# Sample attention: who issues the latent pages

## The reference

```python
def one_seq(args):                                  # 8 sequences
    pages, qb, cb, rb = args
    c_past = cache_kv_latent[pages].reshape(-1, KV_LORA)      # 16 pages x 128 rows x 256
    r_past = cache_k_rope[pages].reshape(-1, QK_ROPE_DIM)
    c_all = jnp.concatenate([c_past, cb], axis=0)[None]       # and the 4 new rows
    k = mla_keys(c_all, r_all, w_uk, g_k_nope, g_k_rope)      # keys, normalised
    p = attn_probs(qb[None], k, mask)
    o_lat = jnp.einsum('bhql,blc->bqhc', p, c_all)            # weighted latent rows
    return jnp.einsum('bqhc,chv->bqhv', o_lat, w_uv)[0]
```

```python
a = gelu(einsum('thkd,td->thk', peer_u[e], hb))     # e: the picked experts of each token
return einsum('thk,thkd->td', (g * a), peer_v[e])
```

## Time and profile before

| | |
|---|---|
| median of 3 runs | 3511.48 us (3498.91 to 3511.61) |
| the profiled execution | 3516.18 us, span 3514.4 us |
| PE busy | 2845.7 us (81%) |
| DVE busy | 2707.2 us (77%) |
| ACT busy | 968.1 us (28%) |
| POOL busy | 1765.9 us (50%) |
| fetches on POOL | 1088 of 1253 (v) and 1329 (u) ns in the mean |
| sample attention | about 863 to 1262 us of the span |

### The profile page before, as it was taken

The page is one execution under the profiler, slowest core; times in us unless marked ns, Lnnn a source line. Parts: engine busy times, 40 slices in busy tenths (PEclk is TensorE's granted clock), DMA queues, the critical chain, the costliest instruction groups (busy, mean ns, idle before and its releaser), DMA issues. The chain is left out here.

```text
span 3514.4 us, 40173 instructions
## 1 busy us (share of the span) xinstructions
PE 2845.7 (81%) x12509; PEld 2094.9 (60%) x12509; DVE 2707.2 (77%) x5283; ACT 968.1 (28%) x1627; POOL 1765.9 (50%) x1379
## 2 busy tenths in 40 slices
PE   6655697886888866656629799999999999999997
PEld 3444354665333333355618677787778777777775
DVE  3237687896878847759979688888888888888886
ACT  2212132432323311111108622222222222222221
POOL 0026455475545526626546445566666555555553
PEclk9677798876989977787859899999999999999998
DMA  3221587687999968830004689899999988999987
GB/s 117 95 107 48 174 286 275 198 303 265 318 314 337 336 236 325 315 114 31 24 2 192 259 312 332 326 345 335 328 333 340 340 316 333 338 338 338 332 320 263
DMA packets 311112, 899.61 MB, mean 256 GB/s; under 512 B 33641, under 2 KB 125082, under 8 KB 300634
## 3 DMA queue, kind: packets, MB, share of 16 engines
q0 software_dynamic: 156672, 570.49, 45.3%
q1 hardware_dynamic: 152266, 323.70, 25.6%
q10 hardware_dynamic: 2016, 3.67, 0.3%
HBM read 844.35 MB, written 53.64 MB: 256 GB/s over the span
## 5 line engine op out<-in xcount | busy, mean ns | idle before, releaser
L126 POOL DMA_INDIRECT x_got<-v,x_expert x544 | 681.6, 1253 | 649.2 <-DVE x_y L148 501.8
L126 POOL DMA_INDIRECT x_got<-u_rows,x_expert x544 | 723.1, 1329 | 541.3 <-DVE x_got L141 392.8
L148 DVE SCALAR_TENSOR_TENSOR x_y<-x_got,x_hidden,x_y 128x1024 f32<-128x1024 f32 x544 | 695.3, 1301 | 44.2 <-DMA x_got<-v,x_expert 35.0
L141 DVE SCALAR_TENSOR_TENSOR x_got<-x_got,x_y 128x1024 f32<-128x1024 f32 x544 | 647.9, 1221 | 36.0 <-DMA x_got<-u_rows,x_expert 34.3
L1783 PE MATMUL e_a<-h2h,e_uh 128*128 128x512 f32 x1024 | 406.9, 397 | 55.6 <-DVE e_ul L1863 35.9
L1784 PE MATMUL e_a<-h2l,e_uh 128*128 128x512 f32 x1024 | 401.2, 392 | 0.0
L1785 PE MATMUL e_a<-h2h,e_ul 128*128 128x512 f32 x1024 | 401.0, 392 | 0.0
L816 PE MATMUL d_kn<-w_uk_kept,d_page 128*128 128x512 f32 x512 | 256.5, 646 | 52.7 <-DMA d_krT<-page_krT 51.9
L1828 ACT ACTIVATE e_vh<-e_v 128x2048 fp32r<-128x2048 f32 x64 | 122.6, 1916 | 585.1 <-PE e_yt L1802 544.8
L1783 PEld LDWEIGHTS e_a<-h2h,e_uh 128*128 128x128 f32 x1024 | 193.5, 189 | 117.1 <-issue 59.2
L1785 PEld LDWEIGHTS e_a<-h2h,e_ul 128*128 128x128 f32 x1024 | 193.7, 189 | 41.4
(11 more groups left out here) (400 smaller groups left out, 5373.2 us busy)
## 6 DMA issues: line engine op xcount, KB each, us to landing
e_u<-uT SPq DMA_DIRECT2D x128, 512.0 KB, 8.4
e_v<-v SPq DMA_DIRECT2D x64, 1024.0 KB
gates_d<-g_stage SPq DMA_DIRECT2D x8, 4096.0 KB, 11.8
e_gate<-gates_d SPq DMA_DIRECT2D x32, 1024.0 KB
d_page<-page SPq DMA_DIRECT2D x128, 144.0 KB, 4.4
d_latent<-page_rows SPq DMA_DIRECT2D x128, 128.0 KB
x_got<-u_rows,x_expert POOLq DMA_INDIRECT x544, 6.2
x_got<-v,x_expert POOLq DMA_INDIRECT x544, 6.2
```

The source lines that it names most:

```text
L126: pool.indirect_dma_start(out=self.got[row][:], out_offset=None, in_=self.tables[phase], in_offset=bass.IndirectOffsetOnAxis(ap=self.exper ...
L141: dve.scalar_tensor_tensor(out=row[:], in0=row[:], scalar=1.0, in1=self.y[g][:], op0=ALU.mult, op1=ALU.mult, accum_out=self.hidden[:, g, k ...
L148: dve.scalar_tensor_tensor(out=self.y[g][:], in0=row[:], scalar=self.hidden[:, g, k:k + 1], in1=self.y[g][:], op0=ALU.mult, op1=ALU.add).t ...
```

## The change

The latent pages and `c_now` are issued by GpSimd. `load_latents` now handles one page; GpSimd's program goes through sequences and pages, issues c_now (at page 0) and the page's latents, and then the fetches that VectorE's steps of that page stand for, still five ahead: by the end the same number of fetches as before. The table read becomes the helper `place_of`, which each engine uses for itself. At page 0 GpSimd waits for `d_lat` of sequence b-2, as SP did. SP keeps the keys, with its wait for the scores; its wait for `d_lat` is gone. Nothing is changed in what is computed or in what the other engines do.

```diff
+        def place_of(eng, b, p):
+            return eng.value_load(table[0:1, bass.ds(b * PAGES + p, 1)], min_val=0, max_val=n_phys - 1)
+
+        def load_latents(eng, b, e, p):
+            if p == 0:
+                after(eng, s["d_lat"], b - 1)
+                eng.dma_start(c_now[e][:], a["kv_all"][bass.ds(SEQ + b * DEC_S, DEC_S), :]).then_inc(latent_in[e], 16)
+            eng.dma_start(latent_rows[e][:, p, :], a["page_rows"][bass.ds(place_of(eng, b, p), 1)]
+                          .rearrange("o p c -> (o p) c")).then_inc(latent_in[e], 16)
+
         @block.sync
...
-            def load_latents(b, e):
-                sp.dma_start(c_now[e][:], a["kv_all"][bass.ds(SEQ + b * DEC_S, DEC_S), :]).then_inc(latent_in[e], 16)
-                for p, phys in each_page(b):
-                    sp.dma_start(latent_rows[e][:, p, :], a["page_rows"][bass.ds(phys, 1)]
-                                 .rearrange("o p c -> (o p) c")).then_inc(latent_in[e], 16)
...
             load_keys(1, 1)
-            load_latents(0, 0)
-            load_latents(1, 1)
             for n in range(1, DEC_B - 1):
                 e = (n - 1) % 2
                 sp.wait_ge(s["d_krsq"], n)
                 sp.wait_ge(s["d_sc"], n)
                 load_keys(n + 1, e)
-                sp.wait_ge(s["d_lat"], n)
-                load_latents(n + 1, e)
...
         @block.gpsimd
         def _(pool):
-            gather.fetch(pool, through)
+            for b in range(DEC_B):
+                for p in range(PAGES):
+                    load_latents(pool, b, b % 2, p)
+                    gather.fetch(pool, through - DEC_B * sum(steps) + b * sum(steps) + sum(steps[:p + 1]))
```

More of the change, by code:

```diff
@@ L754, in sequences, with load_keys @@
                 step()
+        def place_of(eng, b, p):
[6 more added lines that the diff above has]
+                          .rearrange("o p c -> (o p) c")).then_inc(latent_in[e], 16)
         @block.sync
         def _(sp):
-            def each_page(b):
+            def load_keys(b, e):
                 for p in range(PAGES):
-                    yield p, sp.value_load(table[0:1, bass.ds(b * PAGES + p, 1)], min_val=0, max_val=n_phys - 1)
-            def load_keys(b, e):
-                for p, phys in each_page(b):
+                    phys = place_of(sp, b, p)
                     done = first_in[e] if p < FIRST else rest_in[e]
```

## The result

The changed kernel takes 3485.8 us in the median (3479.61 to 3489.64, 4 runs) against 3509.78 (3498.91 to 3511.61, 4 runs) for the kernel before, a ratio of 0.9936 (95% interval 0.9911 to 0.9962). Six more executions beside the experiments gave 3483.93 and a ratio of 0.9926 (0.9908 to 0.9943). By the medians it is faster by 24.0 and 25.2 us, or 0.7%; 95 us slower had been forecast.

A forecast was written before the change was run, and what follows sets the result against it. SP's queue was taken as the bound. With latents moved, GpSimd would become it: +82.8 us for seven sequences and +12.5 for sequence 0, about +95, so 3611, named as 3606 us; range 3480 to 3650.

The forecast's parts named there:

- Step (1), SP relieved: Latents and c_now leave SP's queue: its turn falls from 44.7 to 25.5 us, worth at most 40.7 us.
- The seven waits of 40.7 us: TensorE's waits for late keys in sequences 2 to 7, 40.7 us together, forecast to go.
- Step (2), the price of a page on GpSimd: Latents on GpSimd cost 1.67 us a page, so it needs 57.4 us a sequence: +82.8 us over seven sequences.
- the sign of being wrong that the prediction had named: VectorE's steps still releasing GpSimd's fetches would show its price too high, the stage falling to about 40 us a sequence.
- The structure of the sum: GpSimd's fetches, 16 latent pages and c_now, 30.2 + 16 x + 0.5 us a sequence, set against 45.6, plus sequence 0.
- the formula: Time change from latents on GpSimd over the whole stage: 119 x - 103.5 us, x being the price of a page.
- the turning point of 0.87 us: Price of a latent page on GpSimd at which the forecast change in time is nothing.
- cheap transfers, SP relieved: Rival: read and transfer under about 0.6 us a page on GpSimd, key waits won, 3475 us; chance 0.23.
- the 5 us that I had set aside: Allowance in the cheap rival for a few late fetches, in 3511 - 41 + 5 = 3475.
- Step (2), sequence 0: In sequence 0, GpSimd's added latents delay the last row step from 924.5 to 937.0, +12.5 us.
- Steps (3) and (4): GpSimd passes its wait for d_lat without a stop, 0 us; the last latents cost 0, high bound 3 us.
- the rival that had them held: VectorE holds GpSimd's direct transfers like fetches: 2.06 us a page, 63.7 a sequence, 3653 us; chance 0.10.

The follow-up runs named there:

- e1: The kernel before, but SP takes page numbers as constants and reads no table, still issuing all transfers; 3466.32 us, ratio 0.9875.
- e3: The changed kernel, but GpSimd takes the latents' page numbers as constants and reads no table; 3486.5 us, ratio 0.9925 to the kernel before.
- e6: The changed kernel, but GpSimd issues all 16 latent pages of a sequence at page 0, ahead of the fetches; 3575.24 us, ratio 1.0184 to the kernel before.
- e4: The changed kernel, but each latent page goes in two transfers of 64 rows from GpSimd; 3537.84 us, ratio 1.007 to the kernel before.
- e2: The changed kernel, but ScalarE issues each page's latents behind its square of that page; 3483.38 us, ratio 0.9916 to the kernel before.
- e9: e7, but the latents of sequences 0 and 1 come from GpSimd, page by page; 3483.91 us, ratio 0.9913 to the kernel before.
- e5: The changed kernel, but latent transfers of sequences 2 to 7 bring 16 of 128 rows; 3478.28 us, ratio 0.9906 to the kernel before.
- e11: e9, but from sequence 3 on each latent transfer brings 16 of 128 rows; 3479.97 us, ratio 0.9907 to the kernel before.
- e7: Unlike the changed kernel, SP issues everything, with three latent buffers and, from sequence 2 on, one table read a page; 3494.21 us, ratio 0.9956 to the kernel before.
- e10: e9, but GpSimd first of all issues the 16 krT pages of sequence 0; 3475.05 us, ratio 0.9896 to the kernel before.

## Why the prediction was wrong

**What bounds the kernel: right.** SP's queue paced the stage. e1 shows it: with SP's table reads gone, and the pages read in the order of memory, all key waits vanish and 46.5 us are won.

**Step (1), SP relieved: right.** The seven waits of 40.7 us went; VectorE lost 35.4 us less at the squares.

**Step (2), the price of a page on GpSimd: wrong, and this is what failed.** I took 1.67 us (0.55 read, 0.82 writing, 0.30 gap). The trace has 0.594 + 4.0/128 = 0.63. So GpSimd did not become the bound: VectorE's steps still release fetches, the sign of being wrong that the prediction had named. Each of the three parts was misread.
- The read is hidden (e3: no change without it). I had inferred from the 0.30 us ahead of a released fetch that the sequencer doesn't run ahead. It does: the read of 1011.5 is for a transfer of 1014.50. The 0.30 stands ahead of fetches only; a direct transfer follows a fetch after 0.00. It goes with this kind of instruction, and what it is made of no run shows. In the burst of e6 the read is not hidden, since only direct transfers stand ahead.
- The writing is not "128 rows at the fetch's rate". Transfers of 128, 64 and 16 rows take 0.594, 0.558 and 0.526 us. SP's 0.51 was the nearer row: I chose by the engine where I should have chosen by the kind of instruction.
- The gap of 0.30 had been counted once more per page.

The structure of the sum held. e4 put the page at 1.1 us and cost 25 us where the formula says 27; the turning point of 0.87 us lies between the 0.63 and the 1.1 that were measured on its two sides. With 0.63 the formula gives -28.5, close to the 24.0 and 25.2 us that were won, but not for its reason: it puts GpSimd at 40.8 us a sequence, above VectorE's 39.8, and so still at the bound. In the trace a fetch costs 178.6 / 160 + 0.30 = 1.42 us and not 1.51, which makes 39.0 a sequence of 41.8, and from 920 us on fetches still wait 40.0 us in all for free buffers. So the rival "cheap transfers, SP relieved" is the case. It had a chance of 0.23 and named 3475, 36 under the median of then; the gain was 24.0 and 25.2. The 3485.8 us lie inside the stated range, 3480 to 3650, only because the range was drawn to take in half of this rival.

**Why 25 and not 41.** 40.7 us of TensorE's waits were only 35.4 of VectorE's, and VectorE is what is late next. 10.6 of them came back as rows that came later; the 5 us that I had set aside for that were too few. Two causes were tried. GpSimd's queue: with no latents on it (in e9 from sequence 2 on) the row waits are 16.9 (e2) or 11.0 (e9) against 15.9 and 16.2 in the changed kernel, and the stage is 1.6 and 3.9 us shorter; a small part, and e9 loses some of it to later keys. The DMA engines: with 1.8 MB less a sequence the row waits fall from 16.2 to 12.6 (e5) and from 11.0 to 8.4 (e11), and the sequences by 0.6 and 1.3 us. Both exist in the trace, neither moved the measured time clearly, and the mean of five sequences in one profiled execution is not sharper than this: e7 and e9 issue the same from sequence 3 on and show 40.3 and 41.2. How the two share the 10.6 us is open. So are the 10.0 us by which e1 leads behind its start: it issues its keys in a shorter burst, and it reads key pages that lie one behind the other in memory; neither was tried alone.

**Step (2), sequence 0: wrong with it.** +12.5 had been predicted; its scores start 43.9 us after the first key product, where it had been 43.7. The sum has +5.2 there even at 0.63 a page; why none of it shows is open.

**Steps (3) and (4): as predicted.** GpSimd passes the wait for d_lat without a stop (c_now of 1013.95 follows its fetch at once), and the last latents hold nobody up. GpSimd's queue has two idle stretches of 2.5 and 2.3 us that nothing in the profile releases, one ahead of a latent page at 1021.04 and one ahead of a fetch at 1143.38; they are not at a page 0, and their cause is open. **Step (5):** nothing had been charged for 380 GB/s; 350 to 372 were reached from 920 to 1190 us, and e1 held 382, at landings of 7.8 us and not 6.7. Fetches landed after 7.2 us in the changed kernel, and with fewer bytes (e5) after 6.5, so charging nothing was a little too generous.

**Held transfers.** In the changed kernel fetches last 0.93 to 2.03 us beside VectorE's row steps, direct transfers 0.557 to 0.624, so the rival that had them held is out. That a VectorE instruction with two SBUF inputs gets in the way of a GpSimd instruction that reads SBUF, and not of one that only writes it, is the rule of the Trainium skill, "SBUF — State Buffer", section "Who interferes with whom". The trace agrees, if it is the read of the indices that is held, which no run tested by itself.

**The issuing engine.** Moving the latents to GpSimd or to ScalarE (e2) cost either engine's own work little or nothing, but twice the transfers (e4) cost 49 us against the changed kernel and a burst (e6) some 90. The Trainium skill, "DMA: Bandwidth & Descriptors", section "Issuing engines are not separate DMA queues", calls the sequencer's time to start a transfer usually small beside the transfer. The changed kernel and e2 agree; e1, e4 and e6 show the limit: where the queue is nearly full, that little time is the bound.

## What to carry to other kernels

Look at the queue that issues transfers as at an engine: here 44.7 us of issuing in a 45.6 us period was the bound, though no busy share shows it. When issues move to another queue, multiply instructions, not bytes, add what it already does, and put the new instructions where its own long ones hide their address reads. Subtract positions of two traces only after taking off where the stage begins in each. Price an operation that the trace lacks by the nearest kind of instruction, and when the sign of the answer lies between two nearest rows, say so in the forecast and not only in the range.

## What was unexpected of the hardware

- A direct transfer issued by GpSimd keeps it busy for 0.50 to 0.63 us, and its size matters little: the medians are 0.498 for 16 KB over 32 rows (e10), 0.53 for 16 rows of 1 KB (e5), 0.55 for 64 of them (e4), and for 128 of them 0.54 in a burst (e6) and 0.60 between fetches. An indirect one takes 0.93 at least.
- A table read on GpSimd's sequencer (0.29 load, 0.15 registers) is free behind a fetch (e3) and costs 0.6 us behind a direct transfer (e6).
- GpSimd is idle for at least 0.30 us ahead of every indirect transfer of the stage, even after a direct one.
